# Moving the split of three weight units within the expert passes of a two-layer hybrid decoder trunk

## The chip, the cores and the metric
One core of one Trainium2 chip runs the whole program. The metric is the device time of one execution in microseconds (us), the median over the timed runs of the kernel before. A lower time is better.

## The reference, cut to what matters
The reference runs two decoder layers on 256 tokens of width 1024, in float32. Each layer has a mixer block with four parallel branches and then a mixture of experts (MoE) with 4 groups of 4 experts. The change touches only the MoE, which is this:

```python
def hier_moe(h, w_group, b_group, w_expert, b_expert, w_e_gate, w_e_up, w_e_down):
    t = h.reshape(-1, d)
    g_logits = (t @ w_group + b_group).astype(jnp.float32)
    g_idx = jnp.argmax(g_logits, axis=-1)
    ...
    top_v, top_i = lax.top_k(e_in, TOP_K)
    top_w = jax.nn.softmax(top_v, axis=-1) * g_w
    ...
    hid = jax.nn.silu(jnp.einsum('td,edf->tef', t, w_e_gate)) * jnp.einsum('td,edf->tef', t, w_e_up)
    out = jnp.einsum('tef,efd,te->td', hid, w_e_down, combine.astype(t.dtype))
```

A token chooses one group and then two of the four experts in it. Each expert has a hidden width of 256.

## The kernel before, in words
Every float32 weight is used in two parts so that TensorE can multiply it at its fast rate: `w_hi`, a rounded copy, and `w_lo`, the rest. The weights come in units of 128 x 2048 numbers (1 MB). A unit passes four stations:

1. SyncE issues two DMAs of 512 KB into one slot of a ring (`raw`, and `mid` for slots 4 and 5; six slots in the MoE). It waits until the unit six places earlier has been split.
2. ScalarE (ACT) copies the slot to `w_hi`: the helper `hi(at, n)`, line 522. It waits for the DMA (`landed`) and until TensorE has used the unit four places earlier, since `w_hi` and `w_lo` hold four units (`PART`).
3. VectorE (DVE) subtracts and writes `w_lo`: the helper `lo(at, n)`, line 839. It waits for `hi` of the same unit. Its end frees the DMA slot.
4. TensorE (PE) runs twelve matmuls of 512 columns on the unit: `three`, lines 1380 to 1382. It waits for `split_done`, which `lo` raises.

Each engine has its own instruction stream, written out by hand. The order in a stream is the order of execution, so a waiting instruction holds all that stand behind it on that engine. No planner reorders anything.

The MoE works in passes. A pass takes up to 128 tokens of one group through the group's four experts e = 0 to 3, and reads twelve units, n = 0 to 11: for every expert two gate-and-up units and one down unit. TensorE's order is gate_up(0) with units 0 and 1, gate_up(1) with 2 and 3 and the transposes of hidden(0) between them, down(0) with unit 4, then 5, transposes, 6, down with 7, 8, transposes, 9, down with 10, the transposes of hidden(3), a scatter of the previous pass's result (four small `clear_sums` matmuls in the first pass instead), and down(3) with unit 11.

Between the units the engines do the expert's own work. After gate_up(e), ACT runs `silu(e)` (line 761), DVE multiplies in `hidden(e)` (line 1289), PE transposes (`hidden_tp`, line 1800), ACT copies the transposed block (its own `hidden(e)`, line 766), DVE makes its low part (`hidden_lo(e)`, line 1295), and down(e) uses both. Late in a pass ACT and DVE prepare the tokens of the next one (`pass_tokens`, line 528, and `pass_low`, line 845; the scale `rcur`, line 797). At the end ACT and DVE copy the result out of two PSUM banks (`z_hi`, line 809, and `z_lo`, line 1335), and DVE builds the scatter matrix `sel_t` (line 1332).

"Ahead" in the code is the next pass. Both streams split units 0, 1 and 2 of the next pass before the end of the current one.

The passes of a layer are: the first pass, written out; a loop (`Fori`) over the middle passes; and the last pass, written out (`final`). Ahead of the loop and in each turn of it every engine loads registers from the small table `tab`: ACT loads three ahead of its first looped pass and one in each turn after that, DVE five and three. In the data of this case the first layer has four passes and the second has five.

In front of the first pass of a layer DVE computes routing weights; PE combines them in a few small matmuls (`combine_weights`, lines 1756 and 1760) between units 1 and 2; DVE reads the result (lines 1257 to 1263), and `silu(0)` and `hidden(0)` of the first pass use it.

Of the kernel before, what the change touches and what calls it, by code (L numbers as in the profile page):

```python
# [40 lines left out]
def trunk(nc, x_in, positions, norm1_g, w_in, sgu_ln_g, sgu_ln_b, sgu_w, sgu_b, q_norm_g, k_norm_g, sinks,  # L41
          conv3_w, conv31_w, conv31_b, cnorm_g, cnorm_b, w_branch, w_gate, b_gate, w_o,
          norm2_g, w_group, b_group, w_expert, b_expert, w_e_gate, w_e_up, w_e_down, out):
    DEPTH, D, D_IN = w_in.shape
# [68 lines left out]
    with ExitStack() as ctx:  # L113
# [163 lines left out]
        def S(name):  # L277
            if name not in names:
                names[name] = sem(name)
            return names[name]  # L280
# [233 lines left out]
        def _(act):  # L514
            a = nc.scalar

            def hi(at, n):
                slot = at.raw(n)
                act.wait_ge(landed[slot], at.landed(n))
                act.wait_ge(unit_used, at.ring(n))  # L520
                w = width(n, at.moe)
                a.activation(w_hi[:, at.part(n), 0:w], raw_at(slot)[:, 0:w], ACT.Copy).then_inc(hi_done, 1)  # L522
# [27 lines left out]
            for l in range(DEPTH):  # L550
# [8 lines left out]
                at = At(l, before, False)  # L559
# [194 lines left out]
                def expert_pass(at, PP, tile_next, next_slot, first, final=False):  # L754
                    ahead = At(l, PP + 1, True)

                    def silu(e):
                        act.wait_ge(unit_used, at.unit((1, 3, 6, 9)[e]) + PART + 1)
                        if not first and e == 0:
                            act.wait_ge(S("rcur_done"), PP + 1)  # L760
                        a.activation(sil[:, e % 2, :], bank[6 + e % 2][:, 0:F], ACT.Silu,
                                     scale=rslot[:, 0:1] if first else rcur).then_inc(S("sil_done"), 1)

                    def hidden(e):
                        act.wait_ge(S("hid_tp"), EPG * PP + e + 1)
                        a.activation(hd_hi[:, e % 2, :, :].rearrange("p f s -> p (f s)"), bank[6 + e % 2][:, 0:F],  # L766
                                     ACT.Copy).then_inc(S("hd_hi_done"), 1)


                    if not first:  # L770
                        hi(at, 3)
                    hi(at, 4)
                    act.wait_ge(S("cw_read"), l + 1)
                    silu(0)
                    if first:
                        a.activation(posb[:, :], bank[cw_bank][:, POSB:POSB + SEQ], ACT.Copy).then_inc(S("posb_read"), 1)
                    hi(at, 5)
                    hidden(0)
                    hi(at, 6)
                    silu(1)  # L780
                    hi(at, 7)
                    hi(at, 8)
                    hidden(1)
                    hi(at, 9)
                    silu(2)
                    hi(at, 10)
                    hi(at, 11)
                    hidden(2)
                    if not final or l < DEPTH - 1:
                        hi(ahead, 0)  # L790
                    silu(3)

                    if not final:
                        pass_tokens(0, next_slot, 3 if first else 1)
                        pass_tokens(1, next_slot)
                        act.wait_ge(S("sil_done"), EPG * PP + EPG)
                        a.activation(rcur, rslot[:, tile_next], ACT.Copy).then_inc(S("rcur_done"), 2 if first else 1)
                    hidden(3)
                    if not final or l < DEPTH - 1:
                        hi(ahead, 1)  # L800
                    if not final:
                        hi(ahead, 2)

                    for h in range(2):
                        if h == 0:
                            act.wait_ge(S("y_bank"), PP + 1)
                        else:
                            used(at, 11)
                        a.activation(z_hi[:, 512 * h:512 * h + 512], bank[4 + h][:, :], ACT.Copy).then_inc(S("z_hi_done"), 1)
# [5 lines left out]
                with act.Fori(1, lastp) as p:  # L815
                    tile_next = act.value_load(tab[0:1, 1, bass.ds(p + 1, 1)], min_val=0, max_val=NG - 1)
                    at = At(l, before + p, True)
                    expert_pass(at, before + p, bass.ds(tile_next, 1), tile_next * P, False)
                at = At(l, before + lastp, True)
                expert_pass(at, before + lastp, None, None, False, True)  # L820
                if l < DEPTH - 1:
                    for i in range(2 * T):
# [8 lines left out]
        def _(dve):  # L831
# [70 lines left out]
            for l in range(DEPTH):  # L902
# [305 lines left out]
                at = at_m  # L1208
# [42 lines left out]
                v.tensor_tensor(cmr[:, :, 17], rs2[:, :], cmr[:, :, 16].bitcast(F32), ALU.subtract).then_inc(S("cm_lo_done"), 1)  # L1251
                v.tensor_tensor(cmr[:, :, 8:16], cmf[:, :, :], cmr[:, :, 0:8].bitcast(F32), ALU.subtract).then_inc(S("cm_lo_done"), 1)
                lo(at, 2)
                lo(at, 3)
                dve.wait_ge(S("cw_done"), l + 1)
                cw_ps = bank[cw_bank][:, 0:NG * 18].rearrange("p (g n) -> p g n", g=NG)
                step.mark(v.tensor_copy(cwf[:, :, :], cw_ps))
# [27 lines left out]
                def expert_pass(at, PP, tile, tile_next, cw, first, final=False):  # L1285
                    def hidden(e):
                        dve.wait_ge(S("sil_done"), EPG * PP + e + 1)
                        w = cwf2[:, e:e + 1] if first else cwf2[:, bass.ds(cw * EPG + e, 1)]
                        v.scalar_tensor_tensor(out=hid[:, e % 2, :], in0=sil[:, e % 2, :],
                                               scalar=w, in1=bank[6 + e % 2][:, F:2 * F],  # L1290
                                               op0=ALU.mult, op1=ALU.mult).then_inc(S("hid_done"), 1)

                    def hidden_lo(e):
                        dve.wait_ge(S("hd_hi_done"), EPG * PP + e + 1)
                        v.tensor_tensor(hd_lo[:, e % 2, :, :].rearrange("p f s -> p (f s)"), bank[6 + e % 2][:, 0:F],
                                        hd_hi[:, e % 2, :, :].rearrange("p f s -> p (f s)").bitcast(F32),
                                        ALU.subtract).then_inc(S("hd_lo_done"), 1)

                    if not first:
                        lo(at, 3)  # L1300
                    hidden(0)
                    lo(at, 4)
                    hidden_lo(0)
                    lo(at, 5)
                    hidden(1)
                    lo(at, 6)
                    lo(at, 7)
                    hidden_lo(1)
                    if first:
                        pass_table()  # L1310
                    lo(at, 8)
                    hidden(2)
                    lo(at, 9)
                    lo(at, 10)
                    hidden_lo(2)
                    lo(at, 11)
                    hidden(3)
                    if not final:
                        pass_low(PP, 0, tile_next, 3 if first else 1)
                        pass_low(PP, 1, tile_next)  # L1320
                    hidden_lo(3)
                    ahead = At(l, PP + 1, True)
                    if not final or l < DEPTH - 1:
                        lo(ahead, 0)
                    if not final:
                        lo(ahead, 1)
                        lo(ahead, 2)
                    if not first:
                        dve.wait_ge(S("scattered"), PP)
                    else:  # L1330
                        dve.wait_ge(S("posb_read"), l + 1)
                    v.tensor_scalar(sel_t, posb[:, :], icol[:, tile], None, ALU.is_equal)
                    for h in range(2):
                        dve.wait_ge(S("z_hi_done"), 2 * PP + h + 1)
                        v.tensor_tensor(z_lo[:, 512 * h:512 * h + 512], bank[4 + h][:, :],
                                        z_hi[:, 512 * h:512 * h + 512].bitcast(F32),
                                        ALU.subtract).then_inc(S("selt_done") if h else S("z_half"), 1)
# [6 lines left out]
                with dve.Fori(1, lastp) as p:  # L1344
                    tile = dve.value_load(tab[0:1, 1, bass.ds(p, 1)], min_val=0, max_val=NG - 1)
                    tile_next = dve.value_load(tab[0:1, 1, bass.ds(p + 1, 1)], min_val=0, max_val=NG - 1)
                    cw = dve.value_load(tab[0:1, 2, bass.ds(p, 1)], min_val=0, max_val=2 * NG - 1)
                    at = At(l, before + p, True)
                    expert_pass(at, before + p, bass.ds(tile, 1), tile_next * P, cw, False)

                tile = dve.value_load(tab[0:1, 1, bass.ds(lastp, 1)], min_val=0, max_val=NG - 1)
                cw = dve.value_load(tab[0:1, 2, bass.ds(lastp, 1)], min_val=0, max_val=2 * NG - 1)
                at = At(l, before + lastp, True)
                expert_pass(at, before + lastp, bass.ds(tile, 1), None, cw, False, True)

                for i in range(2 * T):
# [522 lines left out]
```

## Time and profile before

| | us |
|---|---|
| median of 3 runs | 786.16 |
| lowest and highest | 784.63 and 786.23 |
| the profiled execution | 784.63 |
| its span, first to last instruction | 782.9 |

| engine | busy us | share of the span |
|---|---|---|
| PE, matmuls | 772.4 | 99% |
| DVE | 646.9 | 83% |
| ACT | 508.1 | 65% |
| POOL | 22.6 | 3% |

The span is 1.7 us shorter than the profiled execution's time; what lies around the span is not recorded. The share of PE says that matmuls were in flight nearly always. The granted clock of TensorE was 0.999 of full speed. A time below is counted from the start of the span. In the chain of waits, the matmuls are laid end to end, so a start there is the moment from which a matmul held up the next one; it lies about 0.15 us behind the same matmul's start in the list in order of time.

### The profile page before, as it was taken

To read this page: it belongs to the slowest core of one execution; us is meant where nothing else is said; L and a number is where in the kernel's file an instruction comes from. 1 tells how busy PE (TensorE), PEld (TensorE's weight loads), DVE (VectorE), ACT (ScalarE), POOL (GpSimd) and SP (SyncE) were. 2 spreads that over 40 slices of the span, in tenths; PEclk is the share of its full clock that TensorE was granted. 3 is DMA by queue.
4 is the path that set the end of the run, shared out by engine and by line. 5 is a ranking of instruction groups with operands and counts; after the bars stand their busy time and mean duration, and the time that the engine had idled before them with its cause. 6 is when DMAs were issued, how large, how long until landed. Compare 5 with 4: busy or idle time off the path is not lost.

```text
span 782.9 us, 13142 instructions
## 1 busy us (share of the span) xinstructions
PE 772.4 (99%) x4850; PEld 690.5 (88%) x4850; DVE 646.9 (83%) x847; ACT 508.1 (65%) x592; POOL 22.6 (3%) x36
## 2 busy tenths in 40 slices
PE   8999999999999999999999999999999999999997
PEld 7899999999878888888889999999988888888885
DVE  5868898469689999897874799757968998989895
ACT  7625646655588778786643655565569877878772
POOL 4020000000000000000001000000000000000000
PEclk9999999999999999999999999999999999999999
DMA  9867254266719999998365624526562999999971
GB/s 303 273 215 241 83 201 137 94 216 216 269 54 328 346 383 335 386 338 276 119 214 204 225 97 173 162 72 239 212 234 90 334 365 386 336 363 352 354 262 54
DMA packets 79499, 186.76 MB, mean 239 GB/s; under 512 B 12470, under 2 KB 24408, under 8 KB 79448
## 3 DMA queue, kind: packets, MB, share of 16 engines
q1 hardware_dynamic: 79448, 186.08, 67.0%
q8 instruction: 32, 0.52, 0.3%
q14 instruction: 19, 0.16, 0.1%
HBM read 185.01 MB, written 1.05 MB: 238 GB/s over the span
## 4 chain that ended last, share of the span: by engine, by line
PE 96%; DVE 1%; ACT 1%; DMA 1%; issue 1%; POOL 0%; DVEq 0%; SPq 0%; ACTq 0%; POOLq 0%
PE bank L1380 28%; PE bank L1382 28%; PE bank L1381 28%; PE bank L1774 2%; PE bank L1685 2%; PE bank L1800 1%; PE bank L1662 1%; PE bank L1539 1%; DMA x<-in_x 1%; PE bank L1445 1%; PE bank L1448 0%; PE bank L1560 0%; PE bank L1564 0%; PE bank L1655 0%; PE bank L1769 0%
## 5 line engine op out<-in xcount | busy, mean ns | idle before, releaser
L839 DVE TENSOR_TENSOR w_lo<-raw,w_hi 128x2048 fp32r<-128x2048 f32 (+1 forms) x144 | 313.5, 2197 | 56.4 <-ACT w_hi L522 55.8
L522 ACT ACTIVATE w_hi<-raw 128x2048 fp32r<-128x2048 f32 (+1 forms) x144 | 264.1, 1844 | 135.3 <-PE bank L1382 131.4
L1380 PE MATMUL bank<-a_hi,w_hi 128*128 128x256 f32 x688 | 195.8, 285 | 0.6 <-DVE a_lo L905 0.6
L1381 PE MATMUL bank<-a_hi,w_lo 128*128 128x256 f32 x688 | 194.6, 283 | 0.0
L1382 PE MATMUL bank<-a_lo,w_hi 128*128 128x256 f32 x688 | 194.6, 283 | 0.0
L1380 PE MATMUL bank<-w_hi,y_lo 128*128 128x512 f32 x432 | 170.9, 395 | 0.0
L1382 PE MATMUL bank<-w_lo,y_lo 128*128 128x512 f32 x432 | 168.6, 390 | 0.0
L1380 PEld LDWEIGHTS bank<-a_hi,w_hi 128*128 128x128 f32 x688 | 131.9, 192 | 1.6 <-issue 1.5
L1381 PEld LDWEIGHTS bank<-a_hi,w_lo 128*128 128x128 f32 x688 | 132.0, 192 | 0.1
L1382 PEld LDWEIGHTS bank<-a_lo,w_hi 128*128 128x128 f32 x688 | 132.0, 192 | 0.0
L1381 PE MATMUL bank<-w_hi,y_hi 128*128 128x512 f32 x288 | 112.3, 390 | 0.0
L1382 PEld LDWEIGHTS bank<-w_lo,y_lo 128*128 128x128 f32 x432 | 81.1, 188 | 17.0
L1380 PEld LDWEIGHTS bank<-w_hi,y_lo 128*128 128x128 f32 x432 | 81.1, 188 | 16.8 <-issue 0.7
L839 DVE TENSOR_TENSOR w_lo<-mid,w_hi 128x2048 fp32r<-128x2048 f32 x36 | 82.2, 2283 | 0.0
L522 ACT ACTIVATE w_hi<-mid 128x2048 fp32r<-128x2048 f32 x36 | 68.8, 1911 | 4.6 <-PE bank L1382 4.6
L1381 PEld LDWEIGHTS bank<-w_hi,y_hi 128*128 128x128 f32 x288 | 54.2, 188 | 10.4
L1381 PE MATMUL bank<-w_hi,y_lo 128*128 128x512 f32 x144 | 56.0, 389 | 0.0
L1020 DVE SCALAR_TENSOR_TENSOR d_acc<-dpad,pcols,d_acc 128x256 f32<-128x256 f32 x120 | 48.5, 479 | 0.0
L1380 PE MATMUL bank<-w_hi,a_hi 128*128 128x512 f32 (+1 forms) x112 | 42.7, 381 | 0.0
L1382 PE MATMUL bank<-w_lo,a_hi 128*128 128x512 f32 (+1 forms) x112 | 41.9, 375 | 0.0
L1381 PE MATMUL bank<-w_hi,a_lo 128*128 128x512 f32 (+1 forms) x112 | 41.9, 374 | 0.0
L766 ACT ACTIVATE y_lo<-bank 128x256 fp32r<-128x256 f32 x36 | 13.8, 384 | 36.3 <-PE bank L1800 36.3
(309 smaller groups left out, 970.4 us busy)
## 6 DMA issues: line engine op xcount, KB each, us to landing
raw<-in_w_e_gate SPq DMA_DIRECT2D x63, 512.0 KB, 4.9
raw<-in_w_e_up SPq DMA_DIRECT2D x63, 512.0 KB, 6.5
raw<-in_w_gate SPq DMA_DIRECT2D x56, 512.0 KB, 4.5
mid<-in_w_e_down SPq DMA_DIRECT2D x54, 512.0 KB, 6.1
raw<-in_w_in SPq DMA_DIRECT2D x32, 512.0 KB, 6.6
raw<-in_w_e_down SPq DMA_DIRECT2D x18, 512.0 KB, 5.0
raw<-in_w_branch SPq DMA_DIRECT2D x16, 512.0 KB, 4.1
raw<-in_w_o SPq DMA_DIRECT2D x16, 512.0 KB, 4.4
```

Of the source, the lines that this page charges most:

```text
L522: a.activation(w_hi[:, at.part(n), 0:w], raw_at(slot)[:, 0:w], ACT.Copy).then_inc(hi_done, 1)
L766: a.activation(hd_hi[:, e % 2, :, :].rearrange("p f s -> p (f s)"), bank[6 + e % 2][:, 0:F], ACT.Copy).then_inc(S("hd_hi_done"), 1)
L839: v.tensor_tensor(w_lo[:, part, 0:w], raw_at(slot)[:, 0:w], w_hi[:, part, 0:w].bitcast(F32), ALU.subtract).then_inc(split_done, 1)
L1020: last = v.scalar_tensor_tensor(out=d_acc[:, c, :], in0=src, scalar=w, in1=d_acc[:, c, :], op0=ALU.mult, op1=ALU.add)
L1380: mm(ps, a2[0], b2[0], start=first, stop=False, skip_group_check=shared)
L1381: mm(ps, a2[1], b2[0], start=False, stop=False, skip_group_check=shared)
L1382: return mm(ps, a2[0], b2[1], start=False, stop=last, skip_group_check=shared)
L1445: mm(bank[0][:, 256 * f:256 * f + 256], wp[0][:, kk, P * f:P * f + P], hp[:, k, :], start=k == 0 and f == 0 and hp is h_hi, stop=False, sk ...
L1539: return mm(ps, qk_t[r, tq, P * (h % 2):P * (h % 2) + P], qk_t[r, tk, 2 * P:3 * P], start=True, stop=True)
L1662: last = mm(bank[small_bank][:, LG[t]:LG[t] + NR], xr[:, t, c, :], wrs[:, c, :], start=c == 0, stop=c == KT - 1, skip_group_check=True)
L1685: return mm(bank[GT_BANKS[k]][:, :], (xt_hi, xt_lo)[i][t][:, k, :], sel[:, t, :], start=t == 0 and i == 0, stop=t == T - 1 and i == 1)
L1774: last = mm(bank[i][:, :], sel_t[:, P * t:P * t + P], zz[:, 512 * h:512 * h + 512], start=False, stop=zz is z_lo, skip_group_check=True)
```

## The change
In ACT's stream `hi(ahead, 0)` moves from in front of `silu(3)` to behind `pass_tokens`, still in front of `rcur` and of `hidden(3)`. `hi(ahead, 2)` leaves the end of the pass and becomes `hi(at, 2)` at the start of the next one, behind the two `z_hi` copies and, for a looped pass, behind the register loads. In DVE's stream `lo(ahead, 2)` moves likewise: behind `sel_t`, the two `z_lo` and the register loads. In a first pass, `lo(at, 3)` moves from in front of the read of the combined weights to behind it, in front of `hidden(0)`; in the other passes it stays in front of `hidden(0)`. TensorE's and SyncE's streams are the same. No work is added or removed.

```diff
--- before.py
+++ after.py
@@ -786,20 +786,19 @@
                     hi(at, 10)
                     hi(at, 11)
                     hidden(2)
-                    if not final or l < DEPTH - 1:
-                        hi(ahead, 0)
                     silu(3)
 
                     if not final:
                         pass_tokens(0, next_slot, 3 if first else 1)
                         pass_tokens(1, next_slot)
                         act.wait_ge(S("sil_done"), EPG * PP + EPG)
+                    if not final or l < DEPTH - 1:
+                        hi(ahead, 0)
+                    if not final:
                         a.activation(rcur, rslot[:, tile_next], ACT.Copy).then_inc(S("rcur_done"), 2 if first else 1)
                     hidden(3)
                     if not final or l < DEPTH - 1:
                         hi(ahead, 1)
-                    if not final:
-                        hi(ahead, 2)
 
                     for h in range(2):
                         if h == 0:
@@ -815,8 +814,10 @@
                 with act.Fori(1, lastp) as p:
                     tile_next = act.value_load(tab[0:1, 1, bass.ds(p + 1, 1)], min_val=0, max_val=NG - 1)
                     at = At(l, before + p, True)
+                    hi(at, 2)
                     expert_pass(at, before + p, bass.ds(tile_next, 1), tile_next * P, False)
                 at = At(l, before + lastp, True)
+                hi(at, 2)
                 expert_pass(at, before + lastp, None, None, False, True)
                 if l < DEPTH - 1:
                     for i in range(2 * T):
@@ -1251,7 +1252,6 @@
                 v.tensor_tensor(cmr[:, :, 17], rs2[:, :], cmr[:, :, 16].bitcast(F32), ALU.subtract).then_inc(S("cm_lo_done"), 1)
                 v.tensor_tensor(cmr[:, :, 8:16], cmf[:, :, :], cmr[:, :, 0:8].bitcast(F32), ALU.subtract).then_inc(S("cm_lo_done"), 1)
                 lo(at, 2)
-                lo(at, 3)
                 dve.wait_ge(S("cw_done"), l + 1)
                 cw_ps = bank[cw_bank][:, 0:NG * 18].rearrange("p (g n) -> p g n", g=NG)
                 step.mark(v.tensor_copy(cwf[:, :, :], cw_ps))
@@ -1296,8 +1296,7 @@
                                         hd_hi[:, e % 2, :, :].rearrange("p f s -> p (f s)").bitcast(F32),
                                         ALU.subtract).then_inc(S("hd_lo_done"), 1)
 
-                    if not first:
-                        lo(at, 3)
+                    lo(at, 3)
                     hidden(0)
                     lo(at, 4)
                     hidden_lo(0)
@@ -1324,7 +1323,6 @@
                         lo(ahead, 0)
                     if not final:
                         lo(ahead, 1)
-                        lo(ahead, 2)
                     if not first:
                         dve.wait_ge(S("scattered"), PP)
                     else:
@@ -1346,11 +1344,13 @@
                     tile_next = dve.value_load(tab[0:1, 1, bass.ds(p + 1, 1)], min_val=0, max_val=NG - 1)
                     cw = dve.value_load(tab[0:1, 2, bass.ds(p, 1)], min_val=0, max_val=2 * NG - 1)
                     at = At(l, before + p, True)
+                    lo(at, 2)
                     expert_pass(at, before + p, bass.ds(tile, 1), tile_next * P, cw, False)
 
                 tile = dve.value_load(tab[0:1, 1, bass.ds(lastp, 1)], min_val=0, max_val=NG - 1)
                 cw = dve.value_load(tab[0:1, 2, bass.ds(lastp, 1)], min_val=0, max_val=2 * NG - 1)
                 at = At(l, before + lastp, True)
+                lo(at, 2)
                 expert_pass(at, before + lastp, bass.ds(tile, 1), None, cw, False, True)
 
                 for i in range(2 * T):
```

## Rows read from the trace of the kernel before

**Rows 1.** The page: busy time by engine, and the chain of waits by engine.
```profile
PE 772.4 (99%) x4850; PEld 690.5 (88%) x4850; DVE 646.9 (83%) x847; ACT 508.1 (65%) x592; POOL 22.6 (3%) x36
...
PE 96%; DVE 1%; ACT 1%; DMA 1%; issue 1%; POOL 0%; DVEq 0%; SPq 0%; ACTq 0%; POOLq 0%
```
**Rows 2.** DVE in order of time, first pass: start us, duration, line, tiles, idle before.
```profile
232.03 4.49 DVE L839 TENSOR_TENSOR w_lo<-raw,w_hi 128x2048 fp32r<-128x2048 f32 x2
236.44 0.23 DVE L1257 COPY d_acc<-bank 128x72 f32<-128x72 f32 x1
...
237.00 0.19 DVE L1263 TENSOR_TENSOR d_acc<-d_acc 128x32 f32<-128x32 f32 x1
237.81 0.48 DVE L1289 SCALAR_TENSOR_TENSOR gates<-gates,d_acc,bank 128x256 f32<-128x256 f32 x1 [0.61 <-ACT gates L761]
...
250.21 2.29 DVE L839 TENSOR_TENSOR w_lo<-raw,w_hi 128x2048 fp32r<-128x2048 f32 x1
```
**Rows 3.** Chain of waits, first pass of layer one: start us, duration, what.
```profile
235.10 0.79 PE bank L1760 x8
...
238.76 0.22 PE bank L1800 x2
...
252.87 0.23 PE bank L1380
```
**Rows 4.** ACT in order of time, end of the first pass, layer one.
```profile
258.63 0.47 ACT L761 ACTIVATE gates<-bank,d_acc 128x256 f32<-128x256 f32 x1 [0.56 <-PE bank L1382]
...
260.04 0.19 ACT L797 ACTIVATE d_acc<-d_acc 128x1 f32<-128x1 f32 x1
261.57 0.38 ACT L766 ACTIVATE y_lo<-bank 128x256 fp32r<-128x256 f32 x1 [1.33 <-PE bank L1800]
261.85 3.71 ACT L522 ACTIVATE w_hi<-raw 128x2048 fp32r<-128x2048 f32 x2
265.47 1.07 ACT L809 ACTIVATE a_hi<-bank 128x512 fp32r<-128x512 f32 x2
267.83 1.93 ACT L522 ACTIVATE w_hi<-raw 128x2048 fp32r<-128x2048 f32 x1 [1.30 <-issue]
```
**Rows 5.** DVE in order of time, the same stretch.
```profile
261.99 0.42 DVE L1295 TENSOR_TENSOR y_lo<-bank,y_lo 128x256 fp32r<-128x256 f32 x1 [0.57 <-ACT y_lo L766]
...
269.19 1.28 DVE L1335 TENSOR_TENSOR a_lo<-bank,a_hi 128x512 fp32r<-128x512 f32 x2
270.49 2.29 DVE L839 TENSOR_TENSOR w_lo<-raw,w_hi 128x2048 fp32r<-128x2048 f32 x1
```
**Rows 6.** Chain of waits, first to second pass: units 11, 0 and 2 begin.
```profile
262.65 0.43 PE bank L1380
...
265.61 0.23 PE bank L1380
...
271.05 0.23 PE bank L1380
```
**Rows 7.** ACT's first unit split behind the register loads, three of the five boundaries.
```profile
302.28 1.92 ACT L522 ACTIVATE w_hi<-raw 128x2048 fp32r<-128x2048 f32 x1 [0.56 <-issue]
...
636.42 1.92 ACT L522 ACTIVATE w_hi<-raw 128x2048 fp32r<-128x2048 f32 x1 [1.08 <-issue]
...
706.43 1.92 ACT L522 ACTIVATE w_hi<-raw 128x2048 fp32r<-128x2048 f32 x1 [0.44 <-issue]
```
**Rows 8.** Chain of waits: a scatter, and unit 2 beginning in two later passes.
```profile
296.51 1.84 PE bank L1774 x8
...
306.52 0.23 PE bank L1380
...
639.86 0.23 PE bank L1380
```
**Rows 9.** Landing time (us) of unit 8's second DMA, and ACT's split of that unit.
```profile
raw<-in_w_e_up SPq DMA_DIRECT2D x1, 512.0 KB, 7.3
...
279.50 1.92 ACT L522 ACTIVATE w_hi<-raw 128x2048 fp32r<-128x2048 f32 x1 [0.43 <-PE bank L1382]
```

## The prediction
> **What bounds the kernel now.** I read the page first: its busy times and the chain of waits by engine [rows 1]. PE holds 96% of the chain, about 752 of 783 us, and all other engines together have some 30 us, which lie at the start, between the layers and around the router. So inside the expert passes there is next to nothing to win. A change there can only add time, where an engine that fed PE early enough now feeds it too late. The question for each moved instruction is how early its result was there. For that I read the lists in order of time for ACT and DVE [rows 2, 4, 5, 7], where the idle time and its releaser stand in brackets, and set them against the chain [rows 3, 6, 8], where the start of a matmul is the last moment at which its operand may come. Twelve matmuls of one unit take 2.72 us in that chain: units 0 and 1 lie between 265.61 and 271.05 [rows 6]. One unit costs ACT a spacing of 1.82 us (3.71 for two, less the overlap of the last) [rows 4] and DVE 2.20 us (4.49 for two) [rows 2], 2.28 from start to end when it stands alone [rows 5]. A handover from one engine to the next costs 0.03 to 0.04 us: the scatter matrix aside, hidden_lo(3) starts at 261.99, 0.04 behind the end of ACT's copy at 261.95 [rows 4, 5].
>
> **lo(3) behind the read of the weights (two first passes).** Before, DVE used the wait for PE's small matmuls: units 2 and 3 filled 232.03 to 236.44, the read followed at once, and hidden(0) began at 237.81 [rows 2]. PE had finished the weights at 235.10 + 0.79 = 235.89 [rows 3]. After the change DVE has only unit 2 to do ahead of the read. It is done at 234.2 and idles until 235.93. The read's four instructions take 237.19 - 236.44 = 0.75 and end at 236.68; now lo(3) takes 2.20, and hidden(0) runs from 238.91 to 239.39. That is 1.10 us later than before. Its reader is the transposes of line 1800, due at 238.76 [rows 3]. They can start at 239.43, so PE stalls 0.67 us. silu(0) is no obstacle: it waits for the same read and for ACT's hi(4), and it is done well ahead of 238.91. Behind this, DVE works without a pause up to unit 8, so it stays 1.10 late. Unit 8 ended at 250.21 + 2.29 = 252.50 and was due at 252.87 [rows 2, 3]. It now ends at 253.60, is usable at 253.64, and PE, itself late by 0.67, wants it at 253.54: another 0.10. Units 9 to 11 have more room. Both layers have this pattern: 2 x 0.77 = 1.54 us.
>
> **hi(ahead, 0) behind silu(3) and pass_tokens (all passes but the last of a layer).** silu(3) was released by PE [rows 4], not by hi(ahead, 0), so it gains nothing. hi(ahead, 0) now starts at 260.04, where rcur stood. After 1.82 comes rcur, some 0.1 of spacing, and ACT's hidden(3) begins at 261.97 in place of 261.57: 0.40 late. Waiting behind it are hidden_lo(3) on DVE and, for both, down(3) on PE. hidden_lo(3) ran from 261.99 to 262.41; it now ends at 262.81 and is usable at 262.85. Unit 11 was due at 262.65 [rows 6]. The stall is 0.20 us in a first pass, 0.4 for two. In the later passes the cover is longer: the scatter of 1.84 us [rows 8], where a first pass has 1.08 us, from the release of ACT's hidden(3) at 261.57 to 262.65. With 0.7 us more room and 0.2 lacking here, these passes pay nothing. The next pass's units 0 and 1 reach DVE 0.4 later and are due 3 us and more after DVE begins them; that is covered too.
>
> **hi(2) and lo(2) into the next pass (seven boundaries).** No work is added, but it moves past the two z copies and past the register loads, on ACT and on DVE. On ACT the second z_hi waits for the end of unit 11 on PE, 265.61 [rows 6]. Then come the loads: the first split behind them began at 267.83, after 1.30 us of idle time put down to "issue" [rows 4]. Before, that split was unit 3, with 2.7 us more until it was due. Now it is unit 2. hi(2) runs 267.83 to 269.76, lo(2) 269.79 to 272.08, PE may start at 272.12, and unit 2 was due at 271.05 [rows 6]: a stall of 1.07. In the second layer hi(2) starts at 636.42 [rows 7], so lo(2) is usable at 636.42 + 1.92 + 0.03 + 2.28 + 0.04 = 640.69 against 639.86 [rows 8]: 0.83. Together 1.90 us.
>
> At the three boundaries inside the loops ACT has one load in place of three. Its first split starts at 302.28 and lo(2) is usable at 306.55 against a due time of 306.52 [rows 7, 8]: 0.03, so I take nothing from ACT's side. At the two boundaries to a last pass there are no loads on ACT, so there is more room still.
>
> DVE's own loads are not shown. The lower bound is nothing: z_lo ended at 270.47 and the next split began at 270.49 [rows 5]. The upper bound is the time from the end of z_hi, 266.54 [rows 4], to 270.49: 3.95 us for five loads. Counted from the new end of z_hi, about 266.2, this permits lo(2) no later than 270.15 in place of 269.79, so up to 0.4 more there, some 0.6 in layer two, and in the loops (unit 11 ends at 306.52 - 2 x 2.72 = 301.08, z_hi 0.6 later, plus 3.95 is 305.6 in place of 304.23) up to 1.4 at each of three. ACT's nearest rows say less: from the end of unit 11, 2.2 us with three loads and 1.2 with one, so about 0.5 for each load and 0.7 besides. For DVE that is 3.2 and 2.2 us, which end just ahead of ACT's hi(2). I allow 0.1 for each of the five boundaries with loads, 0.5 us, and keep 0 to 5.2 for the range.
>
> On the rule that speaks against this term: the rows show that ACT idled for 1.30, 1.08, 0.56 and 0.44 us behind the z copies [rows 4, 7]. The Trainium skill, "Advanced Engine Details and Errata", section "Sequencer Loop", has the semaphore wait of an engine instruction behind the queue into which the sequencer pushes it, and says that "Other engine instructions can be read & queued while ucode executes". By that rule the loads would be over while z_hi still waits, the boundary would cost nothing, and the sum would be 1.9; by the rows it costs 2.4 and the sum is 4.3. The rows show the idle time, so I go by them.
>
> **What else moves.** The z copies on DVE come some 2 us earlier, but PE needs the banks only at unit 4, so nothing is gained. The slot of unit 2 is freed 3.2 us later (272.08 for 268.9), so SyncE issues unit 8's load later, and unit 9's stands behind it in SyncE's stream. Unit 8 took 7.3 us to land and was split at 279.50 [rows 9]; issued at 272.1, with PE later by 1 us, it lands at about 279.8 at the latest, for a use at 280.6. That is covered, narrowly.
>
> **The sum.** 1.54 + 0.4 + 1.90 + 0.5 = 4.3 us, all on PE's chain. Against the profiled execution of 784.63 (span 782.9 and 1.7 around it) this gives 788.9. That execution was the fastest of three; added to the median of 786.16 it gives **790.5**, which I predict.
>
> **Rivals.**
> A. The register loads are hidden. If they run while z_hi waits, hi(2) starts at 266.2, and what limits lo(2) is DVE: hidden_lo(3) begins at 262.39, 0.34 later unit 0, unit 1, then sel_t and z_lo to 268.7, lo(2) to 270.9, due at 271.05. Only the terms inside the first pass stay: 1.94, so 788.1. Against it stand the idle times of [rows 4, 7]; for it, that in the old order nothing was gained by being early there, so the rows show a start and not its earliest moment. This is the time to which the page's rule above leads.
>
> B. PE has more room than the chain shows, for instance since several semaphores and operand fetches overlap, and stalls of 0.2 to 1 us vanish: 786.2, no change. Against it: the late parts are worked out from instructions that follow each other directly.
>
> C. DVE's loads run at their upper bound, or unit 8 arrives late by DMA in the passes where the loads of the ring run closest. The first adds up to 5.2 - 0.5: 795. The idle-free start at 270.49 [rows 5] bounds but doesn't exclude it.
>
> D. Faster. Before, hi(ahead, 0) waited for its DMA in front of silu(3). In an execution in which that DMA is late, silu(3), hidden(3) on DVE, the transposes and down(3) wait with it; afterwards only unit 0 of the next pass does. It decides when the load lands later than the end of hidden(2), some 2.5 us before silu(3). Its price could be the spread of the runs, 786.16 - 784.63 = 1.5 us: 784.6 if all else is covered. Against it: in the profiled execution silu(3) waited for PE [rows 4].
>
> **How the numbers follow.** Forecast 0.60, with its own range of 788.9 to 792.5; A 0.19; B 0.10; C 0.07; D 0.04. A measurement of this kernel tells 0.2%, 1.6 us, from no change. Faster is D: 0.04. Within 0.2% are B and the part of A in which a median falls near the fastest runs (A itself lies only 0.3 above the bound): 0.15. Slower is the rest: 0.81. Range 787.0 to 793.3: it holds the forecast's, A's and the beginning of C's, and leaves out B and D, most of C and some of A.
>
> **What would show it.** In the first passes: DVE idle before line 1257, waiting for PE; hidden(0) 1.1 us later; an idle PE ahead of line 1800, released by DVE. At the first boundary of each layer: PE waiting for DVE's w_lo by about 1 us, and ACT's hi(2) starting behind "issue". In the first passes' end: a PE wait of 0.2 for hidden_lo(3). Chain of waits: DVE and ACT parts up by some 4 us. The prediction is wrong if DVE has no idle time before line 1257, if hi(2) starts directly behind z_hi, or if PE waits somewhere in the middle of a looped pass.

## The result and the profile after

| | median us | lowest and highest |
|---|---|---|
| before | 786.12 (4 runs) | 784.63 and 786.23 |
| after | 792.91 (4 runs) | 792.05 and 793.75 |

The ratio is 1.0097 with a 95% interval of 1.0075 to 1.0119: the changed kernel is slower, by some 6.8 us in the medians. The prediction had 790.5, which is a ratio of 1.0056 to its median of 786.16, so it had the sign and about 60% of the size. Its range ended at 793.3, a ratio of 1.0091, and the measured ratio lies above that.

An execution's time goes with its mean granted clock (before, 784.4 to 785.0 us at 0.999 or more and mostly 785.9 to 786.7 at 0.997 or 0.998; after, 792.0 to 792.5 and mostly 793.4 to 793.8), so below I also give the "full-clock" time, the median of the executions at 0.999 or more. It is 784.7 before and 792.2 after, a difference of 7.5 us. The two profiled executions had this clock; they took 784.63 and 792.51, with spans of 782.9 and 790.8.

From the profile's page of the changed kernel: busy time by engine, and the chain of waits by engine. They answer to [rows 1].
```profile
PE 774.6 (98%) x4850; PEld 690.0 (87%) x4850; DVE 647.0 (82%) x847; ACT 507.5 (64%) x592; POOL 20.6 (3%) x36
...
PE 86%; DVE 5%; issue 3%; ACT 2%; DVEq 1%; DMA 1%; SPq 0%; POOL 0%; ACTq 0%; POOLq 0%
```
DVE and ACT do the same work as before. The fall of PE's share in the chain, 10%, overstates the loss tenfold: where PE waited for DVE, the chain leaves PE and runs back through several DVE instructions that lay beside matmuls. How long PE waited is read from its own waits: waited for, us in total, times, longest.
```profile
PE bank L1380 <- DVE w_lo L840: 3.5, 5, 1.5
...
PE bank L1800 <- DVE gates L1289: 1.4, 2, 0.7
...
PE bank L1380 <- DVE y_lo L1295: 0.5, 2, 0.3
```
None of these three lines existed before. They are nine waits of 5.4 us in total, all at places that the prediction named: five for unit 2, two at the first transposes of a layer, two at unit 11.

PE in order of time, around three of them:
```profile
239.76 0.44 PE L1800 MATMUL bank<-ident,gates 128*128 128x128 f32 x2 [0.71 <-DVE gates L1289]
...
272.23 0.39 PE L1382 MATMUL bank<-w_lo,y_lo 128*128 128x512 f32 x1
274.11 0.50 PE L1380 MATMUL bank<-w_hi,y_lo 128*128 128x512 f32 x1 [1.49 <-DVE w_lo L840]
274.45 0.39 PE L1381 MATMUL bank<-w_hi,y_hi 128*128 128x512 f32 x1
...
310.19 0.50 PE L1380 MATMUL bank<-w_hi,y_lo 128*128 128x512 f32 x1 [0.31 <-DVE w_lo L840]
```
The same three matmuls at 272 to 274 in the kernel before:
```profile
270.66 0.39 PE L1382 MATMUL bank<-w_lo,y_lo 128*128 128x512 f32 x1
270.89 0.39 PE L1380 MATMUL bank<-w_hi,y_lo 128*128 128x512 f32 x1
271.12 0.39 PE L1381 MATMUL bank<-w_hi,y_hi 128*128 128x512 f32 x1
```
The starts tell more than the bracket. Before, the matmuls start 0.23 us apart, though each lasts 0.39. After, from 272.23 to 274.11 are 1.88 us and from there to the next 0.34. So this wait cost 1.76 us and not 1.49: 0.16 because the matmul ahead no longer overlaps the one that waits, and 0.11 because the next one follows later.

DVE in order of time, first pass and first boundary of layer one (for [rows 2, 5]):
```profile
232.32 2.28 DVE L840 TENSOR_TENSOR w_lo<-raw,w_hi 128x2048 fp32r<-128x2048 f32 x1
236.22 0.23 DVE L1257 COPY d_acc<-bank 128x72 f32<-128x72 f32 x1 [1.62 <-PE bank L1760]
...
237.02 2.29 DVE L840 TENSOR_TENSOR w_lo<-raw,w_hi 128x2048 fp32r<-128x2048 f32 x1
239.23 0.47 DVE L1289 SCALAR_TENSOR_TENSOR gates<-gates,d_acc,bank 128x256 f32<-128x256 f32 x1
...
268.63 1.28 DVE L1333 TENSOR_TENSOR a_lo<-bank,a_hi 128x512 fp32r<-128x512 f32 x2
271.77 4.50 DVE L840 TENSOR_TENSOR w_lo<-raw,w_hi 128x2048 fp32r<-128x2048 f32 x2 [1.86 <-ACT w_hi L522]
```
DVE idles 1.62 us ahead of the read, as forecast (1.7, from 234.2 to 235.93), and again 1.86 us ahead of lo(2). That second idle time is put down to ACT. ACT, at the end of the first pass (for [rows 4]), contradicts it:
```profile
263.13 0.19 ACT L798 ACTIVATE d_acc<-d_acc 128x1 f32<-128x1 f32 x1
263.22 0.37 ACT L766 ACTIVATE y_lo<-bank 128x256 fp32r<-128x256 f32 x1
...
267.22 0.60 ACT L808 ACTIVATE a_hi<-bank 128x512 fp32r<-128x512 f32 x1 [0.77 <-PE bank L1382]
269.41 3.71 ACT L522 ACTIVATE w_hi<-raw 128x2048 fp32r<-128x2048 f32 x2 [1.59 <-issue]
```
hi(2) began at 269.41 and took 1.9 us, so it was over at 271.3. DVE began 0.45 later. What held it is in the chain of waits of that stretch, as DVEq, the sequencer of DVE:
```profile
271.05 0.30 DVEq L1345
271.35 0.03 issue
271.39 0.18 DVEq L1345
...
271.77 2.30 DVE w_lo L840
274.07 0.04 issue
274.11 0.50 PE bank L1380
```
Line 1345 is the last of DVE's register loads. They were on the path.

### The profile page after: what moved, and what is told of

Read it like the earlier page. It is cut to its first block, busy times and chain, and to the rows that moved or that the text cites. A ratio compares the mean times of both kernels' runs of the same rounds, so it can differ in the third digit from the quotient of the medians.

```text
span 790.8 us, 13142 instructions
## 1 busy us (share of the span) xinstructions
PE 774.6 (98%) x4850; PEld 690.0 (87%) x4850; DVE 647.0 (82%) x847; ACT 507.5 (64%) x592; POOL 20.6 (3%) x36
## 4 chain that ended last, share of the span: by engine, by line
PE 86%; DVE 5%; issue 3%; ACT 2%; DVEq 1%; DMA 1%; SPq 0%; POOL 0%; ACTq 0%; POOLq 0%
PE bank L1380 26%; PE bank L1382 25%; PE bank L1381 25%; DVE w_lo L840 3%; PE bank L1685 2%; PE bank L1774 1%; DMA raw<-in_w_in 1%; ACT w_hi L522 1%; PE bank L1800 1%; PE bank L1662 1%; PE bank L1539 1%; ACT y_lo L528 1%; PE bank L1445 1%; PE bank L1448 0%; DVE a_lo L1333 0%
## 5 line engine op out<-in xcount | busy, mean ns | idle before, releaser
L761 ACT ACTIVATE gates<-bank,d_acc 128x256 f32<-128x256 f32 x36 | 16.9, 470 | 31.5 <-PE bank L1382 31.5
```

## The experiments

The kernel before ran beside each group, with a full-clock time of 784.6 to 784.8. Behind each full-clock time stands, in brackets, how many executions it rests on. "Over before" is the difference of the full-clock times.

| label | what is done | median us | ratio to before (95%) | full-clock us | over before |
|---|---|---|---|---|---|
| a_only | only lo(3) behind the read | 787.66 | 1.0028 (1.0017 to 1.0038) | 786.6 (2) | +1.8 |
| b_only | only hi(ahead, 0) later | 785.26 | 0.9998 (0.9990 to 1.0007) | 785.3 (9) | +0.5 |
| c_only | only unit 2 moved | 791.12 | 1.0061 (1.0048 to 1.0074) | 789.7 (2) | +5.0 |
| before_loads | changed kernel, unit 2 ahead of all register loads | 791.48 | 1.0073 (1.0060 to 1.0086) | 789.7 (2) | +4.9 |
| hoisted | changed kernel, two loads earlier | 791.75 | 1.0083 (1.0061 to 1.0106) | 789.6 (1) | +5.0 |
| c_hi_early | c_only, ACT's split ahead of its loads | 791.20 | 1.0089 (1.0063 to 1.0115) | 789.8 (1) | +5.2 |
| c_lo_early | c_only, DVE's split ahead of its loads | 791.96 | 1.0089 (1.0075 to 1.0102) | 791.9 (3) | +7.3 |
| c_dve_loads2 | c_only, DVE's loads doubled | 804.88 | 1.0254 (1.0240 to 1.0269) | none | |
| a_behind_hidden | only lo(3), behind hidden(0) | 789.58 | 1.0042 (1.0021 to 1.0064) | 788.3 (2) | +3.6 |
| c_act_loads4 | c_only, ACT's load four times | 800.88 | 1.0194 (1.0158 to 1.0230) | none | |

**One edit at a time.** Each of the three has one part of the change and nothing else. These are the diffs to the kernel before, cut.

```diff
# a_only
                 lo(at, 2)
-                lo(at, 3)
                 dve.wait_ge(S("cw_done"), l + 1)
...
-                    if not first:
-                        lo(at, 3)
+                    lo(at, 3)
                     hidden(0)
# b_only
-                    if not final or l < DEPTH - 1:
-                        hi(ahead, 0)
                     silu(3)
...
+                    if not final or l < DEPTH - 1:
+                        hi(ahead, 0)
# c_only
-                        hi(ahead, 2)
...
+                    hi(at, 2)
...
-                        lo(ahead, 2)
...
+                    lo(at, 2)
```

> The kernel before with only lo(3) of the first passes moved behind the read of the combined weights. Theory (three separate late handovers): PE waits for hidden(0) at the first transposes of each first pass, 0.87 us each as in the changed kernel, plus about 0.1 at unit 8: +1.9 us on 786.1, so 788.0. Rival (the loss comes from weight slots freed late and so from DMA): no unit 2 is late here, so +0.2 at most.

> The kernel before with only hi(ahead, 0) moved behind silu(3) and the token copies. Theory: hidden_lo(3) is late by 0.3 us at unit 11 in each of the two first passes and in no other pass: +0.6 us. Rival (PE has room there): +0.0. The time hardly tells these apart; the trace's wait at unit 11 does.

> The kernel before with only unit 2's two splits moved into the next pass. Theory: PE waits for unit 2 behind register loads, 1.76 and 1.46 us at the two first boundaries and 0.5 to 0.6 at the three boundaries inside loops, nothing at the two boundaries to a last pass: +4.8 us, 790.9. Rival (the three edits work on each other, PE late from one is late for all): not the remainder of 6.8 - 2.5, but +3 or less, or +6 and more.

In a_only PE waits at the first transposes and, within the passes, nowhere else that it didn't before:
```profile
240.55 0.44 PE L1798 MATMUL bank<-ident,gates 128*128 128x128 f32 x2 [0.71 <-DVE gates L1288]
```
In b_only it waits only at unit 11 of the two first passes:
```profile
262.99 0.47 PE L1381 MATMUL bank<-w_hi,y_lo 128*128 128x512 f32 x1 [0.26 <-DVE y_lo L1296]
```
In c_only it waits five times for unit 2, as long as in the changed kernel:
```profile
PE bank L1381 <- DVE w_lo L839: 3.5, 5, 1.5
```
At full clock the three add up to 7.3 us, where the whole change costs 7.5. The traces say the same more sharply. PE's matmuls are the same 4850 in each kernel, so the start of each can be set against its start in the kernel before, and the difference jumps where PE is held up. In a_only it jumps by 0.93 and 0.93 us at the first transposes of the two layers, in b_only by 0.30 and 0.30 at unit 11, in c_only by 1.76, 0.58, 1.47, 0.54 and 0.51 at unit 2. In the changed kernel the same places have 0.92 and 0.93; 0.30 and 0.30; 1.76, 0.58, 1.47, 0.53 and 0.51.

The theory of three separate late handovers holds, and the edits don't work on each other. The +0.5 of b_only can't be told from nothing by the ratio, but its waits can. No unit 2 is late in a_only and b_only, and they cost what was expected, so DMA is not needed to explain them.

**Unit 2 ahead of the register loads.** Both splits stand directly behind the z copies.

```diff
                         a.activation(z_hi[:, 512 * h:512 * h + 512], ...)
+                    if not final:
+                        hi(ahead, 2)
...
-                    hi(at, 2)
```

(and likewise `lo(ahead, 2)` behind `z_lo` on DVE)

> The changed kernel with unit 2's splits directly behind the z copies, ahead of the register loads, on both engines. Theory (the loads are the cost): hi(2) starts 1.6 us earlier at a first boundary and 0.6 inside a loop, lo(2) starts at the end of z_lo, PE waits for it nowhere; what stays is the first passes' 2.5 us: 788.6. Rival (it is the z copies and the slot that is freed late, not the loads): unit 2 is still late by 0.5 us or more at every boundary, 791 or more.

This expectation failed: at full clock the kernel stays 4.9 us over the kernel before, where the 2.5 us of the first passes were expected to be all. The median, 791.48, even lies where the rival had it, but the rival's late unit 2 isn't there either. PE no longer waits for unit 2, but at the transposes of the next pass. PE's waits, and DVE in order of time:
```profile
PE bank L1800 <- DVE gates L1289: 3.1, 4, 1.0
```
```profile
269.62 2.28 DVE L840 TENSOR_TENSOR w_lo<-raw,w_hi 128x2048 fp32r<-128x2048 f32 x1
273.34 2.29 DVE L840 TENSOR_TENSOR w_lo<-raw,w_hi 128x2048 fp32r<-128x2048 f32 x1 [1.44 <-ACT w_hi L522]
275.55 0.47 DVE L1289 SCALAR_TENSOR_TENSOR gates<-gates,d_acc,bank 128x256 f32<-128x256 f32 x1
```
lo(2) is on time. Its wait for hi(2), which ends at 269.39, holds the sequencer. So the first load starts at 269.44, and they last to 273.25; lo(3) and with it hidden(0) come after them. PE's wait behind them is 0.97 us in layer one and 0.67 in layer two. So the loads cost whatever stands behind them, unit 2 or unit 3. In the kernel before they cost nothing because of where they began. That is seen in the view of one source line, which lists sequencer instructions too (durations in ns, start in us). DVE's first load ahead of the loop, in the kernel before:
```profile
L1342 DVEq TENSOR_LOAD <-tab x1: 545/545/545, 266.6 to 266.6; - x1
```
and the end of the last one:
```profile
L1347 DVEq SEQ_ASSERT  x1: 23/23/23, 270.3 to 270.3; - x1
```
The second z_hi ended at 266.54, and z_lo's wait for it is the last wait ahead of the loads. At that moment DVE itself still worked on lo(2) until 268.93 and then on sel_t and z_lo until 270.47 [rows 5]. The sequencer passed the waits and did 3.7 us of loads under this queued work. The changed kernel took lo(2), 2.2 us of cover, from under the loads and put it behind them.

Behind the loop, ahead of a layer's last pass, DVE has two more loads, of which neither the description of the kernel nor the prediction speaks (lines 1350 and 1351 of the changed kernel). In layer one they run from 341.36 to 342.75 while z_lo is at work until 343.04, and lo(2) begins at 342.98 without idle time. Two loads fit under what is queued, and PE doesn't wait for unit 2 there.

**Fewer loads, and one engine at a time.** If this is so, moving two of the loads ahead of the z copies' waits must remove the wait for unit 2 at the first boundaries, though the slot is still freed late.

```diff
# hoisted, ACT; the same on DVE ahead of sel_t
+                    if first:
+                        act.wait_ge(S("tab_ready"), l + 1)
+                        limits.append(act.value_load(tab[0:1, 0, 6:7], ...))
+                        limits.append(act.value_load(tab[0:1, 0, 5:6], ...))
                     for h in range(2):
...
-                npass = act.value_load(tab[0:1, 0, 6:7], ...)
-                lastp = act.value_load(tab[0:1, 0, 5:6], ...)
+                npass, lastp = limits
```

> The changed kernel with two of the register loads (the number of passes and the last pass) moved, in the first pass, ahead of the waits of the z copies, on ACT and on DVE. Theory (an engine's register loads start only when the wait of its second z copy is over, and unit 2 stands behind them): the loads left take 2.2 us in place of 3.75 on DVE and 0.9 in place of 2.1 on ACT, so PE's wait for unit 2 at the two first boundaries, 1.49 and 1.20 us, goes to about 0, and with it the slow restart: -3.2 us, 789.5. Rival (the late slot and the order of the copies make the wait): 792.5 or more, and the wait stays above 1 us.

PE's waits in this kernel:
```profile
PE bank L1386 <- DVE w_lo L843: 0.8, 3, 0.3
```
Three waits for unit 2 are left, those inside the loops, which the edit doesn't touch; both of the first boundaries are gone, and PE's starts are held up there by 0.24 and 0.21 us in place of 1.76 and 1.47. That is 2.8 us saved, against 3.2 expected. The full-clock time, 2.6 us below the changed kernel's, agrees but is a single execution. The median shows only 1.2 and doesn't settle it: the profiled execution, 792.58, had two stretches at the lower clock level in the mixers, at 94 to 98 and at 467 to 470 us, and each cost PE 1.5 us.

The theory that the late slot and its DMA are the cause of the waits at the first boundaries falls: DVE ends lo(2) at 273.8 here, where it ended at 268.9 before and PE itself runs 2.9 us later, so the slot is still freed later than before, and the wait is gone.

> Only unit 2 moved, with ACT's hi(2) ahead of its register loads and DVE's lo(2) behind its own. Theory (DVE's loads end last, 0.4 us behind ACT's hi(2)): nothing is won over the kernel with only unit 2 moved, +4.5 to +5 us on the kernel before, and PE waits 1.5 and 1.2 us at the first boundaries. Rival (the stall is ACT's loads, as the prediction had it): PE waits nowhere at unit 2, +0.5 at most.

> Only unit 2 moved, with DVE's lo(2) ahead of its register loads and ACT's hi(2) behind its own. Theory (DVE's sequencer stands at lo(2)'s wait for hi(2) and starts 3.75 us of loads only then): PE's wait for unit 2 falls to 1.1 and 0.8 us at the first boundaries, but lo(3) and hidden(0) start at the end of the loads, and PE waits another 1.2 and 1.2 at the transposes: +5.5 us or more, not less than with both behind the loads (+4.8). Rival (DVE's loads are hidden beneath lo(2)): only ACT's part is left, +3.2 us.

```diff
# c_hi_early, ACT                      # c_lo_early, DVE
+    if not final: hi(ahead, 2)        +    if not final: lo(ahead, 2)
...
-    hi(at, 2)                         -    lo(at, 2)
```

Both are c_only with one engine's split placed as in before_loads. With ACT's split early nothing changes: 789.8 at full clock and the same five waits. With DVE's split early the wait for unit 2 falls to 1.08 and 0.86 us, and lo(3) and hidden(0) come late in its place:
```profile
269.87 2.29 DVE L839 TENSOR_TENSOR w_lo<-raw,w_hi 128x2048 fp32r<-128x2048 f32 x1 [1.51 <-ACT w_hi L522]
273.78 2.29 DVE L839 TENSOR_TENSOR w_lo<-raw,w_hi 128x2048 fp32r<-128x2048 f32 x1 [1.61 <-ACT w_hi L522]
275.99 0.47 DVE L1289 SCALAR_TENSOR_TENSOR gates<-gates,d_acc,bank 128x256 f32<-128x256 f32 x1
```
That adds waits of 1.29 and 0.95 at the transposes. Inside the loops, where the list has no new wait, unit 2 and the transposes together still hold PE up by 1.6 us over the three boundaries. So the kernel is slower than c_only, by 2.2 us at full clock. DVE's loads set unit 2's time, and behind ACT's alone it is some 0.4 us less late.

**More loads.** The cost of the loads, by adding some.

```diff
# c_dve_loads2
-    tile = dve.value_load(...); tile_next = dve.value_load(...); cw = dve.value_load(...)
+    (each of the three twice)
# c_act_loads4
-    tile_next = act.value_load(...)
+    (four times)
```

> Only unit 2 moved, and the three loads of each turn of DVE's loop made twice. Theory: three more loads take 1.95 us of DVE's sequencer, all of it on the path, at five boundaries: 9.8 us more than with unit 2 moved alone, so +14.5 on the kernel before, and PE waits 3.4 and 3.1 us at the first boundaries, 2.2 in the loops. Rival (DVE's loads lie beside its queued work and ACT's end last): less than 1 us more at each boundary, +10 at most.

> Only unit 2 moved, and ACT's one register load in each turn of its loop made four times. Theory (both engines' loads are serial behind the z copies; DVE's end 0.4 us behind ACT's hi(2), so that much of ACT's is free): three loads of 0.45 us make hi(2) 1.35 later and unit 2 0.95 later at each of five boundaries, waits of 2.4 and 2.15 at the first boundaries and 1.2 in the loops, 4.75 us on top of the kernel with unit 2 moved alone, so +9.9 on the kernel before at the same clock. With DVE's loads doubled, waits above 2 us were followed by some 3 us at the lower clock level; if that holds here the two first boundaries cost another 1.4 each. Rival (only DVE's loads are on the path): +5.2.

PE's waits, first with DVE's loads doubled, then with ACT's load four times:
```profile
PE bank L1384 <- DVE w_lo L839: 12.7, 5, 3.4
```
```profile
PE bank L1384 <- DVE w_lo L842: 9.9, 5, 2.7
```
With DVE's loads doubled the waits were 3.35 and 3.03 at the first boundaries and 2.15, 2.11 and 2.09 in the loops: 9.2 more than in c_only for 15 more loads, 0.61 us each, where 0.65 were expected. With ACT's load four times (15 more loads as well) they were 2.69, 2.44 and 1.65 to 1.54, 6.4 more in place of the 4.75 expected. ACT idled 3.20 us ahead of hi(2), so its loads took 0.54 each and not 0.45. Both engines' loads count, ACT's after its first 0.4 us.

The times rose by more than the waits: 20 us over the full-clock time before with DVE's loads doubled, where 14.5 were expected, and 16 with ACT's, where 9.9 were (12.7 with the clock). The rest is in the granted clock. The columns of this view are: stretch, its length, busy time of PE, PEld, DVE, ACT and POOL, granted clock, DMA share, GB/s. DVE's loads doubled, first boundary:
```profile
274.00:275.00 1.00, 0.51 (x1) 0.50 (x2) 1.00 (x2) 1.00 (x1) 0.00 (x0) 0.58 0.00 0
276.00:277.00 1.00, 1.00 (x4) 0.81 (x3) 1.00 (x3) 0.00 (x0) 0.00 (x0) 0.50 0.94 291
277.00:278.00 1.00, 1.00 (x4) 0.79 (x4) 1.00 (x2) 0.00 (x0) 0.00 (x0) 0.71 1.03 361
278.00:279.00 1.00, 1.00 (x8) 0.78 (x7) 1.00 (x1) 0.00 (x0) 0.00 (x0) 1.00 0.98 254
```
and PE in order of time:
```profile
275.93 0.63 PE L1384 MATMUL bank<-w_hi,y_lo 128*128 128x512 f32 x1
276.36 0.63 PE L1385 MATMUL bank<-w_hi,y_hi 128*128 128x512 f32 x1
...
277.62 0.39 PE L1385 MATMUL bank<-w_hi,y_hi 128*128 128x512 f32 x1
277.85 0.40 PE L1386 MATMUL bank<-w_lo,y_lo 128*128 128x512 f32 x1
```
PE stood still for 3.35 us, and then the clock lay at the lower of its two levels, 1.2 GHz, until about 277.6. At that level the matmuls started 0.43 us apart, and 0.23 apart again from 277.62 on. By PE's starts such a stretch behind a wait cost 1.4 to 1.7 us on top of what the wait costs. With DVE's loads doubled there are four of them, some 6 us. In the profiled execution with ACT's load four times there are two behind waits and a third at 94 to 98 us, in the mixer, away from the change; with it, that execution's time is accounted for.

**lo(3) one place further.**

```diff
# a_behind_hidden, first pass
-                    lo(at, 3)
                     hidden(0)
+                    lo(at, 3)
                     lo(at, 4)
```

> The kernel before with lo(3) of the first passes behind hidden(0), one place further than in the changed kernel. Theory (DVE has 1.6 us of idle time ahead of the read that lo(3) used to fill, and pays its 2.2 us afterwards to whoever needs it first): hidden(0) is early again and PE doesn't wait at the transposes; it waits for unit 3 instead, whose lo(3) ends near 240.2 where it is due at 238.98, so 1.2 us and a slow restart in each layer: +3.0 us on the kernel before. Rival (it is hidden(0)'s lateness alone that costs): +0.3 at most.

The wait went where expected, to unit 3: 1.25 us in layer one, 1.20 in layer two, longer than the 0.71 at the transposes.
```profile
242.07 0.50 PE L1381 MATMUL bank<-w_hi,y_lo 128*128 128x512 f32 x1 [1.25 <-DVE w_lo L839]
```
At unit 8 PE is held up by another 0.16 and 0.22, which no other kernel here shows to more than 0.06. At full clock the kernel takes 3.6 us more, where 3.0 were expected. So it isn't hidden(0) as such that pays, but the 2.2 us of DVE work that no longer lies in its idle time.

## Why the prediction was wrong in size

Two steps failed, both sizes of terms whose place was right. The sum took each stall of PE at its bare length, which lost 1.9 us. And it took DVE's register loads to be over ahead of ACT's hi(2), which lost 1.1 us.

**What bounds the kernel.** Right. No part of the change gained anything, and each microsecond of new wait came out in the time.

**lo(3).** Right: hidden(0) was forecast 1.10 us late with a wait of 0.67, and the wait is 0.71. Of the added 0.10 at unit 8 the starts show nothing in layer one and 0.05 in layer two. PE had been held up 0.22 longer at the transposes than the wait itself, which gives DVE that much room.

**hi(ahead, 0).** Right: a stall of 0.20 was forecast, and 0.25 and 0.26 measured (0.30 each by the starts), in the first passes alone.

**hi(2) and lo(2), ACT's side.** Right. On the chain as it was, hi(2) was put 2.22 us behind the end of unit 11, and it came 2.23 behind it.

**hi(2) and lo(2), DVE's side.** This step failed. It said "DVE's own loads are not shown", bounded them by 0 and 3.95 us from the end of z_hi, and took "about 0.5 for each load" from ACT, hence 3.2 and 2.2 us, an allowance of 0.1 for each boundary. They were shown, in the view of one source line: 266.6 to 270.3 in the kernel before, the whole of the upper bound, because DVE started them at the moment its last wait was over. From one of these loads to the next are 0.62 to 0.73 us, and 0.90 behind the first of layer one. The waits for unit 2 are 1.49 and 1.20 where 1.07 and 0.83 were forecast, and 0.31, 0.27 and 0.24 where 0 was: 3.5 us for 1.9 and an allowance of 0.5. So the upper bound, "up to 0.4 more there, some 0.6 in layer two", was the right value in layer one (0.42 more) and too high in layer two (0.37 more); inside the loops, at "up to 1.4", it was far too high. The loop boundaries, put at 0.03 from ACT's side, came out 0.24 to 0.31 late for the same reason.

**A term that was missing.** The prediction put the cost of a stall beyond its length at nothing, without a reason, and this is the larger of the two misses. In the chain the matmul behind a wait for unit 2 holds the next one up by 0.50 us in place of 0.23, and the two transposes together take 0.44 in place of 0.22 [rows 3]. Five times 0.27 and twice 0.22 are 1.8 us. Some 0.16 of it at each wait is in how the due times were read: they came from the chain, where unit 2 is due at 271.05, but the list has that matmul's start at 270.89.

| place | forecast us | waits listed | PE later by the starts |
|---|---|---|---|
| transposes of the first passes | 1.54, with unit 8 | 1.42 | 1.85 |
| unit 11 of the first passes | 0.4 | 0.51 | 0.60 |
| unit 2, first boundaries | 1.90 | 2.69 | 3.23 |
| unit 2, inside the loops | 0.5, for all five boundaries | 0.82 | 1.62 |
| sum | 4.3 | 5.4 | 7.3 |

The spans differ by 7.9. Of this 0.3 was there ahead of the first pass, where PE waits in the mixer for 0.6 us in place of 0.3 (line 1445), and 0.3 comes in pieces below 0.1 between these places.

**The rivals.** A, loads hidden while z_hi waits, falls: the first loads start at 265.7 on ACT and 266.6 on DVE, just as unit 11 and z_hi end. The section "Sequencer Loop" in "Advanced Engine Details and Errata" of the Trainium skill has the sequencer push engine instructions into a queue. With this the trace agrees: DVE's loads ran from 266.6 beside work queued until 270.47. The prediction's reading of that section, that the loads would run while z_hi still waits, doesn't come out of the trace: here each wait is an instruction of its own in the stream, and the loads begin within 0.05 us of the end of what was awaited (266.54 and 266.58 in the kernel before), and in before_loads and c_lo_early behind lo(2)'s wait. C's first half was the better description of DVE's loads at layer one's first boundary, but its 795 was not reached; its DMA half has no support, since the waits at the first boundaries vanish in hoisted. B falls, since the forecast stalls are in the trace, but for the 0.10 at unit 8. D falls with b_only, which has its edit and gains nothing at full clock: the spread that D priced goes with the granted clock.

## What to carry to other kernels

Before a piece of work is moved past register loads or any other work of the sequencer, ask what the engine had queued while its sequencer did them. That cover goes with the work, and the loads then stand bare in front of whatever comes next. Look for the sequencer's instructions in the view of their source line, where idle time is put down to another engine's result that came earlier. And where TensorE had no idle time, add to each new wait what its listed length leaves out, here 0.2 to 0.3 us.

## What had not been expected of the hardware

DVE's register loads of one number took 0.55 us for the first TENSOR_LOAD of layer one and about 0.3 for the others, with 0.18 to 0.21 of register arithmetic behind each.

With added loads, four of the five waits with DVE's loads doubled and the two longest with ACT's were followed by some 3 us at 1.2 GHz; the other waits were not. With DVE's loads doubled, waits of 2.15 and 2.11 were followed by it and one of 2.09 was not, so no length of wait that brings it can be read from these runs. In other executions a stretch at the lower level lay in the mixer or the router, away from the change. The windows of c_only show one:
```profile
95.00:100.00 5.00, 5.00 (x34) 5.00 (x34) 5.00 (x5) 3.72 (x17) 0.00 (x0) 0.73 0.33 91
```
Ahead of it, from 88.8 to 94.4, PE had run the mixer's short matmuls of 128 columns, as it did in the kernel before, which shows no such stretch there. Across it PE falls 1.5 us behind the kernel before. Why one execution has such a stretch and the next hasn't, no run here tells.
